# Pick rounds over a tile's own columns only, all in the first pass, and a split load of keys and values, in a hybrid decoder step

## The reference

```python
def index_scores(q_i, k_i, w_i):
    s = jnp.einsum('bthd,bsd->bths', q_i, k_i, preferred_element_type=jnp.float32) * (IDX_DIM ** -0.5)
    return jnp.einsum('bths,bth->bts', jax.nn.relu(s), w_i.astype(jnp.float32))
...
        sc = index_scores(qib, k_i, wib)
        sc = jnp.where(kpos[None, None, :] <= qpos[None, :, None], sc, -jnp.inf)
        vals, idx = lax.top_k(sc, topk)
        ks = jax.vmap(lambda kk, ii: kk[ii])(k_b, idx)
        vs = jax.vmap(lambda vv, ii: vv[ii])(v_b, idx)
        return sparse_attend(qb, ks, vs, vals > -jnp.inf)
...
    h, gate = modulate(xp, c_prompt, g_norm[l], w_ada[l], b_ada[l])
    (q_a, k_a, v_a, z_a, q_b, k_b, v_b, z_b, q_i, k_i, w_i, g_a, g_b) = in_proj(h, w_in[l], pos_p)
    o_a = dilated_prompt(q_a, k_a, v_a)
    o_b = dsa_prompt(q_b, k_b, v_b, q_i, k_i, w_i)
```

## Time and profile before

| | us |
|---|---|
| median of 3 runs | 3094.94 |
| lowest, highest | 3093.84, 3099.76 |
| the profiled execution, its own time | 3101.24 |
| its span, first to last instruction | 3099.7 |
| TensorE busy | 2902.5 |
| VectorE busy | 2065.1 |

### The profile page before, as it was taken

One profiled execution on the slowest core, in us unless ns is written; L12 is line 12 of the kernel. 1 busy time (PEld: TensorE's weight loads), 2 busy tenths in 40 slices (PEclk: granted clock), 3 DMA queues, 4 the chain that ended last, 5 costly groups with the idle time before them and its releaser, 6 DMA issues. The chain is left out here.

```text
span 3099.7 us, 56860 instructions
## 1 busy us (share of the span) xinstructions
PE 2902.5 (94%) x21627; PEld 2718.9 (88%) x21635; DVE 2065.1 (67%) x2884; ACT 1076.3 (35%) x1830; POOL 1051.2 (34%) x1057
## 2 busy tenths in 40 slices
PE   5979999999999999999888899899989999999998
PEld 4848999999999999899888899788876988998986
DVE  4586889887778778887676764266644644654755
ACT  5233323232222332222333334475432323333333
POOL 3164666643333354444344344242133110010000
PEclk8999999999999999999999999999999999999999
DMA  9934454454544566666677766684379784683772
GB/s 347 359 126 139 144 174 153 157 162 139 154 150 125 200 160 153 172 164 159 184 189 193 192 166 156 200 244 121 109 211 298 206 293 125 200 273 116 218 236 95
DMA packets 433850, 570.52 MB, mean 184 GB/s; under 512 B 32580, under 2 KB 330244, under 8 KB 430596
## 3 DMA queue, kind: packets, MB, share of 16 engines
q1 hardware_dynamic: 408646, 481.79, 49.4%
q0 software_dynamic: 23888, 84.58, 11.8%
q10 hardware_dynamic: 1152, 2.13, 0.2%
HBM read 418.98 MB, written 151.53 MB: 184 GB/s over the span
## 5 line engine op out<-in xcount | busy, mean ns | idle before, releaser
L3084 PE MATMUL banks<-h_hi,wc_lo 128*128 128x272 f32 x4256 | 1237.2, 291 | 0.0
L3084 PEld LDWEIGHTS banks<-h_hi,wc_lo 128*128 128x128 f32 x4256 | 811.3, 191 | 0.0
L3082 PE MATMUL banks<-h_hi 128*128 128x272 f32 x2432 | 713.2, 293 | 69.8 <-DVE col L2884 56.3
L3083 PE MATMUL banks<-h_lo,h_hi 128*128 128x272 f32 x2432 | 709.8, 292 | 0.0
L3082 PE MATMUL banks<-h_hi,wc_hi 128*128 128x272 f32 x1824 | 530.6, 291 | 15.4 <-ACT col L2725 8.6
L3082 PEld LDWEIGHTS banks<-h_hi 128*128 128x128 f32 x2432 | 466.4, 192 | 77.3 <-issue 65.5
L3083 PE MATMUL banks<-h_lo,wc_hi 128*128 128x272 f32 x1824 | 527.9, 289 | 0.0
L3083 PEld LDWEIGHTS banks<-h_lo,h_hi 128*128 128x128 f32 x2432 | 467.2, 192 | 0.0
L2725 ACT COPY col<-banks 128x544 f32<-128x544 f32 x304 | 186.4, 613 | 717.2 <-PE banks L3084 568.5
L3082 PEld LDWEIGHTS banks<-h_hi,wc_hi 128*128 128x128 f32 x1824 | 345.4, 189 | 20.7 <-issue 16.5
L3083 PEld LDWEIGHTS banks<-h_lo,wc_hi 128*128 128x128 f32 x1824 | 346.0, 190 | 0.0
(11 more groups left out here) (334 smaller groups left out, 5419.6 us busy)
## 6 DMA issues: line engine op xcount, KB each, us to landing
raw<-in_w_in SPq DMA_DIRECT2D x76, 1024.0 KB, 6.5
scratch_proj<-col SPq DMA_DIRECT2D x120, 544.0 KB, 4.2
u_raw<-in_w_out SPq DMA_DIRECT2D x96, 512.0 KB, 5.1
ada_w<-in_w_ada SPq DMA_DIRECT2D x16, 2048.0 KB, 14.2
u_raw<-in_w_pb SPq DMA_DIRECT2D x48, 512.0 KB, 4.8
col<-scratch_proj POOLq DMA_DIRECT2D x44, 544.0 KB, 7.4
scratch_proj<-col POOLq DMA_DIRECT2D x32, 544.0 KB, 7.5
gate_w<-in_w_ada SPq DMA_DIRECT2D x16, 1024.0 KB, 5.9
```

The source lines that it names most:

```text
L3082: nc.tensor.matmul(dst, hi[:, j, :], high, start=(fresh and j == 0), stop=False, skip_group_check=True)
L3083: nc.tensor.matmul(dst, hi[:, j, :], low, start=False, stop=False, skip_group_check=True)
L3084: mm = nc.tensor.matmul(dst, lo[:, j, :], high, start=False, stop=(j == KB - 1), skip_group_check=True)
```

## The change

Rounds read and write only the columns that their tile may see (`seen`), and `PICK_ROUNDS` is keyed by step and gap. All seven tiles lie in steps 1 to 36: tile 0 in steps 1 to 3, tile 1 in 4 to 7, tile 2 in 8 to 11, tile 3 in 12 to 16, tile 4 in 17 to 22, tile 5 in 23 to 29, tile 6 in 30 to 36. The rounds of a step are spread over its gaps, gap 0 left out in a tile's first step and gap 3 in its last. The second pass has none. The third range of keys and values is loaded in two portions: the odd heads after the last step's P4, ahead of `kiT` in SyncE's queue, and the even heads where all stood before.

```diff
+        PICK_AT = [range(1, 4), range(4, 8), range(8, 12), range(12, 17), range(17, 23), range(23, 30), range(30, 37)]
         PICK_ROUNDS = {}
-        for x in range(5):
-            for y in range(7):
-                PICK_ROUNDS[2 + 7 * x + y] = (x, 5 - y % 2)
-        for x in range(2):
-            for y in range(16):
-                PICK_ROUNDS[PAIRS + 1 + 17 * x + y] = (5 + x, 2)
...
+        for x, steps in enumerate(PICK_AT):
+            for y, s in enumerate(steps):
+                n = (y + 1) * ROUNDS_ALL // len(steps) - y * ROUNDS_ALL // len(steps)
+                spots = (1,) if n == 1 else (1, 2, 3) if y == 0 else (0, 1, 2) if y == len(steps) - 1 else (0, 1, 2, 3)
+                for z, spot in enumerate(spots):
+                    PICK_ROUNDS[s, spot] = (x, (z + 1) * n // len(spots) - z * n // len(spots))
...
+        KV_LOADS = (5 * 16, 5 * 16, 9 * 16)
...
-            def load_keys_values(x):
+            def load_keys_values(x, heads=slice(0, None)):
...
-                    sp.dma_start(dst[:, :, a:b], proj[first:first + n, :, a:b].rearrange("m p n -> p m n"))\
+                    sp.dma_start(dst[:, heads, a:b], proj[first:first + n][heads, :, a:b].rearrange("m p n -> p m n"))\
                         .then_inc(kv_landed[x], 16)
...
             load_keys_values(0)
             load_keys_values(1)
+            sp.wait_ge(p_done, done(LAST, "P4"))
+            load_keys_values(2, slice(1, None, 2))
             sp.wait_ge(ki_stored, 16)
             sp.wait_ge(p_done, done(LAST, "P5"))
...
             sp.wait_ge(p_done, done(LAST, "P7"))
-            load_keys_values(2)
+            load_keys_values(2, slice(0, None, 2))
...
-        def pick_round(dve):
-
-
-            nc.vector.max(best8[:], work[:])
+        def pick_round(dve, x):
+
+            seen = work[:, 0:WIDTH_OF(PICKS[x])]
+            nc.vector.max(best8[:], seen)
             dve.drain()
-            nc.vector.match_replace(work[:], best8[:], work[:], TAKEN)
+            nc.vector.match_replace(seen, best8[:], seen, TAKEN)
             dve.drain()
...
-            for c in range(parts[n]):
-                pick_round(dve)
-            if last and n == (3 if all_ == 2 else 2):
-                picked(dve, x + 1)
+            if (s, n) in PICK_ROUNDS:
+                x, times = PICK_ROUNDS[s, n]
+                if s == PICK_FIRST[x] and n == 1:
+                    dve.wait_ge(work_landed, 16 * (x + 1))
+                for c in range(times):
+                    pick_round(dve, x)
+                if s == PICK_LAST[x] and (s, n + 1) not in PICK_ROUNDS:
+                    picked(dve, x + 1)
```

More of the change, by code:

```diff
@@ L489, in decode_step @@
         ROUNDS_ALL = TOPK // 8
+        PICK_AT = [range(1, 4), range(4, 8), range(8, 12), range(12, 17), range(17, 23), range(23, 30), range(30, 37)]
         PICK_ROUNDS = {}
-        for x in range(5):
-            for y in range(7):
-                PICK_ROUNDS[2 + 7 * x + y] = (x, 5 - y % 2)
-        for x in range(2):
-            for y in range(16):
-                PICK_ROUNDS[PAIRS + 1 + 17 * x + y] = (5 + x, 2)
-        PICK_STEPS = [[s for s in PICK_ROUNDS if PICK_ROUNDS[s][0] == x] for x in range(7)]
-        assert all(sum(PICK_ROUNDS[s][1] for s in steps) == ROUNDS_ALL for steps in PICK_STEPS)
-        PICK_FIRST, PICK_LAST = [x[0] for x in PICK_STEPS], [x[-1] for x in PICK_STEPS]
+        for x, steps in enumerate(PICK_AT):
[4 more added lines that the diff above has]
+                    PICK_ROUNDS[s, spot] = (x, (z + 1) * n // len(spots) - z * n // len(spots))
+        assert all(sum(n for y, n in PICK_ROUNDS.values() if y == x) == ROUNDS_ALL for x in range(len(PICK_AT)))
+        PICK_FIRST, PICK_LAST = [x[0] for x in PICK_AT], [x[-1] for x in PICK_AT]
         assert PICK_LAST[-1] < STEPS - 1
@@ L2910, in rounds @@
                 rotate(dve, ROT_IN[s, n])
-            if s not in PICK_ROUNDS:
-                return
-            x, all_ = PICK_ROUNDS[s]
-            at_steps = PICK_STEPS[x]
-            late, last = s == at_steps[0], s == at_steps[-1]
-            parts = (0, 1, 0, 1) if all_ == 2 else (0, 1, 2, all_ - 3) if late else (2, all_ - 3, 1, 0) if last else (1, 1, 1, all_ - 3)
-            if late and n == 1:
-                dve.wait_ge(work_landed, 16 * (x + 1))
-            for c in range(parts[n]):
-                pick_round(dve)
-            if last and n == (3 if all_ == 2 else 2):
-                picked(dve, x + 1)
+            if (s, n) in PICK_ROUNDS:
[6 more added lines that the diff above has]
+                    picked(dve, x + 1)
         def dve_step(dve, s):
```

4 lines of the change are left out of this document (2 added, 2 removed).

## The result

| | before | after |
|---|---|---|
| median beside each other, 4 runs each, us | 3097.35 | 3134.34 |
| lowest, highest | 3093.84, 3104.99 | 3129.87, 3138.16 |
| profiled execution, its span | 3101.24, 3099.7 | 3134.92, 3133.4 |

Medians compare runs on the same chip. The change makes the kernel slower: ratio 1.0116, 95% interval 1.0098 to 1.0134. The direction was the one forecast, the size was not: 37 us instead of 12, and outside the range.

What follows compares the result with a forecast made beforehand. TensorE, busy 94% of the span, was taken as the bound, with VectorE late at certain places. First pass +16.6, steps 54 and 55 -5, portions 0 sum to +11.6; 3094.9 + 11.6 gives 3106 us, range 3083 to 3120.

Steps and rivals of the forecast that it cites:

- the 64 rounds that leave the second pass at nothing: Second pass: removing the rounds gains nothing, since VectorE would only idle longer ahead of rotations; no round in the loop.
- a rival: GpSimd's transfer of col starts 2.8 us sooner and slows rot_x or col's store: 22 steps lose 1 us each, 3128, chance 0.08.
- the page's rule that stood beside the rival: DMA engines alternate between queues packet by packet, so the earlier transfer takes half the engines from what the loop waits for.
- 12 taken: First pass, tiles 0 to 3: TensorE's added waits for VectorE, taken as 12 us between at least 9.1 and 26.
- +16.6: First pass: added waits of 12 + 2.5 - 0.7 = 13.8 us, at 1.2 us of time per us waited.
- the window with nothing unused: First pass: VectorE's time per tile of k steps, 21.11 k - 6.78 us, set against its rounds, picked and other work.
- 1.3 us a step lost: First pass: up to 8.9 us in 7 steps of VectorE's window can't be used, as it waits for products.
- its lower bound of 3.3: First pass, tile 0 in 3 steps: VectorE's demand of 59.9 us exceeds its window of 56.6 by 3.3.
- its two terms: Steps 54 and 55: -5 us, bounds -7 and 0, from removing the store of picks and the next tile's load.
- The first term: Step 54: without the picked tile's store, the next load no longer stands 9.7 us behind the rotation's store; 3.5 us gained.
- The portions: Keys and values in two portions behind the projection: 0 us, bounds -5 and +2; part of the wait moves to kiT.
- the forecast of 11.6: Whole kernel: +16.6 - 5 + 0 = +11.6 us, giving 3106; forecast's chance 0.55, own range 3097 to 3118.

Runs made afterwards that it cites:

- Held back in either way: Against the change: GpSimd's first accumulating transfer waits for rot_x in steps 57 to 67, 3109.43 us; or one round put back in gap 3 of steps 56 to 67, 3112.14 us.
- a kernel that had it: The change with six tiles in the first pass, 3083.78 us; with two rounds in gap 1 instead of one each in gaps 1 and 3, 3113.46 us.
- narrow rounds with the old table: The kernel before with rounds over a tile's own columns and nothing else changed: 3088.05 us against 3099.74, ratio 0.9962.
- the kernel with the transfer held back: The change, with GpSimd's first accumulating transfer in steps 57 to 67 issued only when rot_x has landed: 3109.43 us, ratio 1.0041.

## Why the prediction was right or wrong

**The step that failed** is "the 64 rounds that leave the second pass at nothing; their cover is these idle times of 1 to 4 us, each ahead of a rotation". It holds in steps 43 to 53, which changed by less than 2 us. VectorE's wait for rot_x there was 39.7 us in the earlier trace rows and is now

```profile
DVE rot_x L2895 <- DMA rot_x<-scratch_proj: 98.6, 20, 7.0
```

so the 22 rounds of 2.78 us that left, 61.2 us, became idle time almost whole, as predicted. No store of col is issued in those steps, before or after. It fails for the round in gap 3. That one stood ahead of the sum for which GpSimd's transfer waits, and the order of that transfer and SyncE's store of col hung on it. Held back in either way, 25.7 or 24.4 of the 26.4 us are gone; taken out of gap 3 in a kernel that had it, 32.6 us come. The prediction had the mechanism as a rival, with the 2.8 us and the row, at a chance of 0.08 and 1 us a step over 22 steps. It was 2.4 us a step over 11: I had spread a small cost over all rotation steps instead of asking in which of them the transfer would change places with another one. The two issue times stood 2.2 us apart in the trace before, and the round that left took 2.78. That comparison would have given the change of order, and step 56 of the same trace had its price: a store of col of 7.5 us.

Of the page's rule that stood beside the rival (the Trainium skill, DMA: Bandwidth & Descriptors, arbitration by turns between queues), the runs show what it would lead one to expect: the store of col lands 7.7 us after its issue when the other transfer is ahead, 4.4 when it comes 2.2 us later. Turns packet by packet are not seen in these rows, and whether they alone would make 0.4 us behind (step 61, 4.2 us) so different from 0.2 us ahead (5.1 and 7.2 us) is open.

**The first pass** was right in mechanism and place: the largest wait at step 12, MAX8 at 384 columns 0.56 us against 0.55. The waits of 12.75 us against 12 taken are in part luck, since the 12 was picked between 9.1 and 26. Two sizes were off. The waits grew by 15.0 us instead of 13.8: 12.75 less 0.70 in steps 3 to 18, and 3.0 in steps 19 to 37 (8.13 for mod_t instead of 6.24, 1.78 for col instead of 0.68). And a microsecond of wait cost 24.0 / 15.0 = 1.6 instead of 1.2; the prediction's own rows of the second pass had given 1.43. So +16.6 should have been +24.0. What the prediction did not see at all is that the kernel before lost 9.4 us at mod_t already, which narrow rounds with the old table give back. Tile by tile, the waits behind tiles 1 to 3, 2.02, 6.62 and 1.86 us, lie between the window with nothing unused (2.8 under, 5.8 over, level) and with 1.3 us a step lost. Tile 0's 2.25 is below its lower bound of 3.3. VectorE's subtractions of low parts took 10.0 us in steps 1 to 3, against 13.8 before, where the prediction gave every step the same 6.53 us of other work.

**Steps 54 to 56** gave -6.6 against -5. The kernels that exchange no tile at steps 54 and 55 have 63 to 65 us in steps 54 to 56, with or without a round in step 56, and those that do have 71.6 to 73. So the place was right, but one of its two terms was misread. The 14.24 us of the earlier trace rows were put down to the load of the next tile. In step 56 of the change nothing is loaded, and the store of col still takes 7.2 us, against 7.5 before; in both GpSimd's transfer is ahead of it, by 0.3 and 0.7 us. In the kernel with the transfer held back, whose added wait begins only behind this step, it happens to come 0.4 us behind the store; the store takes 4.5 us, and the step has no wait. The first term, the store of the picks, holds in part: the next load stands 5.9 us behind the rotation's store instead of 9.7. These kernels also lack the rounds of step 54, and no run takes the two apart.

**The portions** gave nothing, as predicted, and the 10.0 us wait was split in two (10.1 in the change).

**The tail** is 8.5 us shorter in the pair of profiles. It is not the portions: the kernel that has only these shows 1123.4, and nine others that have them 1118.6 to 1123.6. Single executions of the same tail differ by as much as that, and why is open. The medians differ by 37.0 us, the profiles by 33.7. The profiles are thus 22.1 us above the forecast of 11.6: 26.4 from steps 57 to 67, 7.4 from the first pass, -1.6 each from steps 38 to 53 and 54 to 56, and -8.5 from the tail. Without the tail, which no one foresaw, the miss would be larger.

## What to carry to other kernels

Before work is taken from an engine that is not the bottleneck, list who waits for the instruction behind it, and which transfers start then: compare the issue times of neighbouring transfers on all queues with the time that is removed. If a removal makes two of them change places, the order is worth stating by a wait instead of by chance; here one wait was worth 23 to 25 us. And separate an edit into its parts on the chip: narrow rounds alone were worth 0.4%, the first pass's table that came with them cost twice that, and the emptied gap as much again. With one tile left in the second pass and fewer rounds at each tile's end the same idea runs in 3076.6 us against 3097.3, 0.6% faster than before.

## What the hardware showed that I had not expected

A short wait of TensorE can cost nearly twice itself, and does not always. At step 8 it waited 2.02 us; these are the windows from the first product behind it.

```profile
412.60:413.90 1.30, 1.27 (x10) 1.30 (x11) 1.30 (x3) 0.00 (x0) 0.00 (x0) 0.98 0.66 268
413.90:417.10 3.20, 3.20 (x16) 3.20 (x16) 0.41 (x1) 0.00 (x0) 0.00 (x0) 0.50 0.65 212
417.10:420.00 2.90, 2.90 (x24) 2.90 (x23) 0.00 (x0) 1.13 (x2) 1.29 (x1) 0.97 0.98 240
```

The granted clock falls to 0.50, its level of 1.2 GHz, 1.3 us after TensorE is busy again, stays there for 3.2 us and returns; the step is 3.8 us longer. At step 4 the wait was 2.25 us, and the step is 2.5 us longer. There the clock stayed at 1.00 behind the wait:

```profile
325.90:345.00 19.10, 19.09 (x152) 19.10 (x153) 13.74 (x25) 5.27 (x9) 9.55 (x9) 1.00 0.67 220
```

In steps 57 to 67, with waits of 0.7 to 5.5 us in every step, the mean clock is 0.91 in the change, 0.96 before.

More work can make a program faster: 12 useless rounds, 26 us of VectorE's time, took 22 us off the time of the changed kernel.
